# Seven waits of a two-block transformer kernel set in another order

## The reference, cut to what matters

```python
def rmsnorm(x, g):
    y = xf * lax.rsqrt(jnp.mean(xf * xf, axis=-1, keepdims=True) + EPS)
    return (y * g)
def swiglu(u, w_gate_up, w_down):            # F = 2816, four times in all
    gate, up = jnp.split(u @ w_gate_up, 2, axis=-1)
    return (jax.nn.silu(gate) * up) @ w_down
# block 1
h = x + 0.5 * swiglu(rmsnorm(x), ...)                       # ffn0
h = h + merged(rmsnorm(h)) @ w_mix_out                      # mix
h = h + memory_cross_attention(rmsnorm(h), rmsnorm(mem))    # xq, xo
h = h + 0.5 * swiglu(rmsnorm(h), ...)                       # ffn1
x = rmsnorm(h)
# block 2, layer 0: delta rule and memory attention, then FFN; layer 1: windowed attention
x = x + concat(gated_delta_rule(...), memory_attention(...)) @ w_out[0]   # qkv, gz, wo0
x = x + swiglu_2(rms_norm(x), ...)                          # ffn2
kv = rms_norm(x) @ w_kv ; shared_k = apply_partial_rope(k, cos, sin)
x = x + concat(sliding_window_attention(...), memory_attention(...)) @ w_out[1]   # q1, mq1, wo1
x = x + swiglu_2(rms_norm(x), ...)                          # ffn3
return rms_norm(x)
```

## Time and profile before

| | before |
|---|---|
| median of three runs | 1583.55 us (1582.07 to 1584.06) |
| profiled execution | 1582.77 us, span 1580.9 us |
| PE busy | 1538.4 us, 97% of the span |
| POOL busy | 1179.8 us, 75% |
| ACT busy | 836.7 us, 53% |
| DVE busy | 585.6 us, 37% |
| mean granted PE clock | 0.993 |
| DMA | 259.77 MB, mean 164 GB/s |

### The profile page before, as it was taken

The page is one execution under the profiler, slowest core; times in us unless marked ns, Lnnn a source line. Parts: engine busy times, 40 slices in busy tenths (PEclk is TensorE's granted clock), DMA queues, the critical chain, the costliest instruction groups (busy, mean ns, idle before and its releaser), DMA issues.

```text
span 1580.9 us, 21595 instructions
## 1 busy us (share of the span) xinstructions
PE 1538.4 (97%) x8592; PEld 1333.2 (84%) x8592; DVE 585.6 (37%) x992; ACT 836.7 (53%) x1310; POOL 1179.8 (75%) x508
## 2 busy tenths in 40 slices
PE   9999999999999999999999999999999998999997
PEld 7888789999888889878888888987888787778886
DVE  3111019356885612331231686452115246311101
ACT  6444464375666445365454685445444375554443
POOL 8889688888667889388878876627887872288893
PEclk9999999999999999999999999999999999999999
DMA  7555555565645555265555543015555451255551
GB/s 266 188 181 201 163 193 182 184 202 188 199 134 184 171 177 189 85 212 186 182 194 193 183 154 116 2 62 177 186 183 200 150 174 54 86 181 187 185 198 43
DMA packets 71859, 259.77 MB, mean 164 GB/s; under 512 B 7984, under 2 KB 8784, under 8 KB 71504
## 3 DMA queue, kind: packets, MB, share of 16 engines
q1 hardware_dynamic: 69408, 250.44, 47.8%
q10 hardware_dynamic: 2352, 7.96, 1.4%
HBM read 257.29 MB, written 1.08 MB: 163 GB/s over the span
## 4 chain that ended last, share of the span: by engine, by line
PE 84%; DVE 6%; POOL 5%; ACT 4%; issue 1%; POOLq 0%; ACTq 0%; DVEq 0%
PE bank L551 14%; PE bank L553 14%; PE bank L552 14%; PE bank L521 5%; PE bank L523 5%; PE bank L522 5%; POOL w_lo L436 5%; PE bank L581 4%; PE bank L583 4%; PE bank L582 4%; PE bank L694 1%; ACT w_hi L1323 1%; PE bank L1073 1%; PE bank L1094 1%; PE bank L1241 1%
## 5 line engine op out<-in xcount | busy, mean ns | idle before, releaser
L436 POOL TENSOR_TENSOR w_lo<-raw,w_hi 128x1024 fp32r<-128x1024 f32 x469 | 1132.8, 2443 | 345.2 <-ACT w_hi L1323 345.0
L1323 ACT ACTIVATE w_hi<-raw 128x1024 fp32r<-128x1024 f32 x474 | 486.8, 1057 | 379.1 <-PE bank L553 182.4
L551 PE MATMUL bank<-w_hi,u_hi 128*128 128x512 f32 x880 | 349.6, 397 | 7.8 <-POOL w_lo L436 7.8
L553 PE MATMUL bank<-w_hi,u_lo 128*128 128x512 f32 x880 | 343.9, 391 | 0.0
L552 PE MATMUL bank<-w_lo,u_hi 128*128 128x512 f32 x880 | 343.5, 390 | 0.0
L551 PEld LDWEIGHTS bank<-w_hi,u_hi 128*128 128x128 f32 x880 | 165.6, 188 | 43.7 <-POOL w_lo L436 9.4
L521 PE MATMUL bank<-u_hi,w_hi 128*128 128x256 f32 x688 | 197.8, 287 | 1.7 <-DVE ones_at L2366 1.7
L553 PEld LDWEIGHTS bank<-w_hi,u_lo 128*128 128x128 f32 x880 | 165.6, 188 | 35.4
L523 PE MATMUL bank<-u_hi,w_lo 128*128 128x256 f32 x688 | 195.4, 284 | 0.0
L522 PE MATMUL bank<-u_lo,w_hi 128*128 128x256 f32 x688 | 195.3, 284 | 0.0
L552 PEld LDWEIGHTS bank<-w_lo,u_hi 128*128 128x128 f32 x880 | 165.8, 188 | 32.7
(11 more groups left out here) (418 smaller groups left out, 2096.1 us busy)
## 6 DMA issues: line engine op xcount, KB each, us to landing
raw<-in_w SPq DMA_DIRECT2D x474, 512.0 KB, 4.4
bc<-acs_scratch ACTq DMA_DIRECT2D x8, 512.0 KB, 5.8
mem_t<-in_mem ACTq DMA_DIRECT2D x2, 1024.0 KB, 6.2
out<-out_t SPq DMA_DIRECT2D x4, 256.0 KB, 2.8
xf<-in_x ACTq DMA_DIRECT2D x1, 512.0 KB, 8.2
xf<-in_x SPq DMA_DIRECT2D x1, 512.0 KB, 8.8
lvl<-in_lvl ACTq DMA_DIRECT2D x1, 448.0 KB, 5.4
band<-in_band ACTq DMA_DIRECT2D x1, 256.0 KB, 5.4
```

Source lines behind the costliest of these rows:

```text
L436: nc.gpsimd.tensor_tensor(w_lo[:, q % RAW, :], raw[:, q % RAW, :], w_hi[:, q % HI, :].bitcast(F32), ALU.subtract).then_inc(split_done, 1)
L551: mm(b[:], hi[:, kt, a], w_hi[:, q % HI:q % HI + 2, c], start=kt == 0, stop=False)
L553: m = mm(b[:], lo[:, kt, a], w_hi[:, q % HI:q % HI + 2, c], start=False, stop=kt == KT - 1)
L1323: fn(w_hi[:, q % HI, :], raw[:, q % RAW, :], ACT.Copy).then_inc(hi_made, 1)
```

## The change

Seven edits, all in the order of waits and instructions; no operation is added or dropped except for one wait that becomes several.

1. `acc_stage`: PE waits for the low part of each held-back piece just ahead of its first use.
2. ffn2's end, ACT: the last `hid_hi` comes ahead of the sines, and five more weight high parts (`after(P0["ffn2_down"] + 4)`) too. DVE: the zeroing of kz and vz comes after the last `hid_lo`.
3. `qkv`: the wait for `picks` comes after the third row tile.
4. `half_tiles`: the second token half goes through k-tiles 0, 1, 2, 3, 6, 7, 4, 5.
5. `hi_part` gets `fed_to`: the weight high parts that were made after the eight high parts of u are made after the fourth. So for ffn1, ffn2 and ffn3; for mix one more of them comes even before the first.
6. Second attention, ACT: `normalise(i - 1)` comes ahead of head i's exponential.
7. Second attention, DVE: `rope(3)` comes ahead of `row_max(8)`.

```diff
@@ acc_stage @@
-                pe.wait_ge(split_done, P0[name] + n)
                 ready(n - 1)
                 for d in range(2):
                     for q in range(n - tail, n):
+                        if d == 0:
+                            pe.wait_ge(split_done, P0[name] + q + 1)
                         m = part(q, 0, d)
@@ PE, delta rule @@
-            pe.wait_ge(W["picks"], 2)
             for j in range(9):
                 row_stage("qkv", u_hi, u_lo, sub=(j, 1))
+                if j == 2:
+                    pe.wait_ge(W["picks"], 2)
...
-                    first, last = kt == (6 if s else 0), kt == (5 if s else 7)
+                    first, last = kt == 0, kt == (5 if s else 7)
...
-            half_tiles(1, (6, 7, 0, 1, 2, 3, 4, 5))
+            half_tiles(1, (0, 1, 2, 3, 6, 7, 4, 5))
@@ ACT @@
-            def hi_part(name, s, gain, dst=u_hi, turn=None):
+            def hi_part(name, s, gain, dst=u_hi, turn=None, fed_to=None):
+
                 for kt in range(KT):
+                    if kt == 4 and fed_to:
+                        after(fed_to)
...
                 after(d - 1)
+                if f == 2:
+                    hid_hi(f, 10)
                 if before_down:
                     before_down()
-                hid_hi(f, 10)
+                if f != 2:
+                    hid_hi(f, 10)
...
-            after(P0["gate_a"] - 5)
-            hi_part("mix", 0, "mix_norm")
-            after(P0["gate_a"] - 3)
+            after(P0["gate_a"] - 4)
+            hi_part("mix", 0, "mix_norm", fed_to=P0["gate_a"] - 3)
...
-            hi_part("ffn1", 0, "ffn2_norm")
-            after(P0["xo"] + 5)
+            hi_part("ffn1", 0, "ffn2_norm", fed_to=P0["xo"] + 5)
...
             def sines():
+                after(P0["ffn2_down"] + 4)
...
             for i in range(16):
+                if i:
+                    normalise(i - 1)
                 act.wait_ge(W["at_max"], h2 + i + 1)
...
-                if i:
-                    normalise(i - 1)
@@ DVE @@
-                dve.wait_ge(piece_done, P0["ffn2_down"] + 16)
-                for t in (kz, vz):
-                    v.memset(t[:], 0.0).then_inc(W["zeroed"], 1)
             ffn(2, beside_zeros)
+            dve.wait_ge(piece_done, P0["ffn2_down"] + 16)
+            for t in (kz, vz):
+                v.memset(t[:], 0.0).then_inc(W["zeroed"], 1)
...
+                if i == 6:
+                    rope(3)
                 if i + 2 < 16:
                     row_max(i + 2)
-                if i in (2, 6):
-                    rope(2 if i == 2 else 3)
+                if i == 2:
+                    rope(2)
```

More of the change, by code:

```diff
@@ L1801, in _ @@
             square("ffn2", 0)
-            hi_part("ffn2", 0, "ln_ffn_a")
-            after(P0["wo0"] + 5)
+            hi_part("ffn2", 0, "ln_ffn_a", fed_to=P0["wo0"] + 5)
             def ffn2_early():
@@ L1870, in _ @@
             square("ffn3", 0)
-            hi_part("ffn3", 0, "ln_ffn_b")
-            after(P0["wo1"] + 5)
+            hi_part("ffn3", 0, "ln_ffn_b", fed_to=P0["wo1"] + 5)
             def ffn3_early():
```

## The result

| | after |
|---|---|
| median of four runs | 1556.82 us (1555.94 to 1559.13) |
| kernel before, beside it | 1583.80 us median of four |
| ratio after to before | 0.9839 (95% interval 0.9826 to 0.9852) |
| profiled execution | 1559.13 us, span 1557.3 us, mean clock 0.997 |

Faster by 25.5 us by the ratio (23 to 28); forecast were 1561.0 us and 1556 to 1570.

What follows compares the result with a forecast made beforehand. TensorE (PE) was taken as the bound, busy 97% of the span, leaving only its waits and clock to win. Terms summed to 23.1 us, less 0.6 given back: 1583.55 - 22.5 = 1561.0 us, range 1556 to 1570.

Steps and rivals of the forecast that it cites:

- tails, first and third FFN: Ends of the first and third FFN's down projections: piecewise waits remove two PE waits of 0.94 us, 1.9 us.
- ffn2's end: End of ffn2's down projection: with the sines later, PE's 3.31 us wait goes entirely, plus 1.7 us of clock.
- picks: First qkv row tile: PE's 1.74 us wait on DVE's ones_at goes, plus 1.7 us of clock, 3.4 us.
- wo0's order: Delta rule's output: high part released two tiles earlier, 1.36 us off PE's 1.92 us wait, plus 1.7 us of clock.
- ffn1 to ffn3: Starts of the three FFNs: low part 1.0 us earlier, PE back 0.9 us earlier each, 2.7 us; bounds 0 and 3.1.
- mix: Start of mix: earlier weight high parts shorten the first gap, but later adds delay PE; net loss 0.65 us.
- attention: Second attention: normalising and rotation moved earlier leave 3.1 of 9.0 us idle, 5.9 us won, plus 1.7 us of clock.
- clock steps: Four PE stretches at the lower clock, 1.7 us each, vanish with the gaps ahead of them.
- Rival (c): Everything goes as walked and mix's gaps shrink too: 1557.6 us, chance 0.10.
- A gap that goes takes its clock loss along: PE's clock: assumed that removing an idle gap also removes the lower-clock stretch behind it, 1.7 us each.
- Rival (a): Waits go but clock steps stay, meeting remaining gaps elsewhere: 16.3 us won, 1567.2 us; chance 0.27 shared with another rival.
- the 0.6 that I gave back: Whole kernel: 0.6 us taken off the summed gain for a clock step one of the remaining gaps may find.

Runs made afterwards that it cites:

- x_tails: Changed kernel with PE again waiting once, for the last low part, ahead of a down projection's held-back pieces: 1561.28 us, ratio to before 0.9869.
- x_picks: Changed kernel with the wait for the one-hot columns (picks) again ahead of the first qkv row tile: 1560.35 us, ratio to before 0.9863.
- y_norms: Changed kernel with weight high parts again behind all eight high parts of u in ffn1, ffn2 and ffn3, mix left changed: 1560.07 us, ratio 0.9868.
- the second measurement: Changed kernel run again unaltered, beside the kernel before: medians 1557.50 and 1581.18 us, ratio 0.9851.
- x_ffn2end: Changed kernel with ACT's sines and DVE's zeroing at ffn2's end in their old places, piecewise waits kept: 1558.50 us, ratio to before 0.9849.
- y_att: Changed kernel with the second attention's old order on both ACT (normalising) and DVE (rotation): 1566.42 us, ratio to before 0.9909.
- z_before: The kernel before the change, run once more unaltered: 1581.51 us, ratio to before 0.9997.
- z_order: Changed kernel with wo0's second token half again in k-tile order 6, 7, 0, 1, 2, 3, 4, 5: 1558.58 us, ratio to before 0.9850.

## Why the prediction was right, step by step

| term | predicted, us | measured, us | from |
|---|---|---|---|
| tails, first and third FFN | 1.9 | 2.5 | 1.25 each, x_tails |
| ffn2's end | 3.3 | 3.5 | PE's starts, before and after |
| picks | 1.7 | 1.9 | gap 1.74 and the start behind it, x_picks |
| wo0's order | 1.4 | 1.3 | 1.92 to 0.60 |
| ffn1 to ffn3 | 2.7 | 2.9 | y_norms |
| mix | -0.65 | -0.2 | PE's starts, before and after |
| attention | 5.9 | 7.4 | 9.1 over the stage, less 1.7 for its step |
| clock steps | 6.8, less 0.6 | 5.3 | 1.5, 1.6, 1.7 and 1.7, less 1.2 at kv |
| last turn at the higher clock | 0 | 0.6 | PE's starts, before and after |
| sum | 22.5 | 25.2 | last matmul: 25.2 |

The last turn has no term in the prediction. The step at the rotation is put at its full 1.7 us; if it cost less, the attention's gaps are worth as much more. The execution gives 23.6, for the slower write at its end. By the runs' medians it is 27.0, by the ratio 25.5, in the second measurement 23.7: two executions compared part by part don't say which of these is the change's.

**The gaps** went where the walk had them, by the instruction it named; that each term came back alone when its part was undone shows it. ffn2's end is the closest walk. DVE, ACT and POOL there, after:

```profile
1210.55 2.37 DVE L2610 TENSOR_SCALAR ang<-ang 128x256 f32<-128x256 f32 x1
1212.96 2.37 DVE L2611 TENSOR_SCALAR ang<-ang 128x256 f32<-128x256 f32 x1
1215.37 0.29 DVE L2612 TENSOR_SCALAR ang<-ang 128x256 f32<-128x256 f32 x1
...
1232.79 0.68 DVE L1939 TENSOR_TENSOR h_lo<-bank,h_hi 128x512 fp32r<-128x512 f32 x1
...
1216.48 0.42 ACT L1825 ACTIVATE cs<-ang 128x256 f32<-128x256 f32 x1 [3.11 <-DVE ang L2614]
...
1217.93 28.99 POOL L436 TENSOR_TENSOR w_lo<-raw,w_hi 128x1024 fp32r<-128x1024 f32 x12 [2.75 <-ACT w_hi L1325]
```

Shifted by the 9.4 us won up to there, the walk said ACT back at 1216.6, POOL at 1217.7, the last hidden low part at 1233.6; the rows have 1216.48, 1217.93 and 1232.79. Seven of DVE's ten last angle steps took 2.4 to 2.5 us, the two-source ones too (three in 7.58 us at 1202.94), and the three behind POOL's pause 0.29 to 0.43. That agrees with the rule of the Trainium skill (SBUF — State Buffer, Who interferes with whom) for both kinds of step, the single-source ones and those with two SBUF inputs.

What was wrong there is the booking, which changed the total by 0.2 us only: the sum gave the sines edit 3.31 us and a step, and the piecewise waits nothing at this place, though it used them itself to cover a last low part 1 us late (1.55 by the row: 11 low parts from 1217.93 end at 1244.5, the tail starts at 1242.97). x_ffn2end shows what that hid: with the waits in, the edit is worth 0.95 us, a third of it the zeroing's move on DVE.

**Sizes off.** ffn1 to ffn3: each turn of x was to be 0.3 us late for DVE's later add. In ffn3 the add ran from 1360.90 to 1361.58 and the turn began at 1361.64, with no bracket, but 0.41 us after the start of the matmul ahead of it; in the kernel before it was 0.24. In all 0.2 us are lost there, near the 0.3. The 2.9 us lie within the bounds of 0 to 3.1. Attention: 3.1 us were to remain (0.1, 0.8, 0.6, 1.1, 0.5), and 2.4 do (0, 0.87, 0.18, 0.81, 0.49). y_att's own waits there are 8.9 us, so 6.6 of its 7.4 are waits; the last 0.8 are stalls too small for a row, which I hadn't walked. Mix: the edit against itself costs 0.2 and not 0.65. The first gap came out as walked (1.56, predicted 1.6), but the turn lost 0.35 us (no bracket) instead of 0.5 and the product behind it 0.5 (bracket 0.41) instead of 0.7. The tails were put at their brackets, 0.94 us, and are worth 1.25 each. Rival (c)'s gain isn't there either, though its 1557.6 is the number nearest to the median.

**The clock** is the step that was right for a reason that doesn't hold as stated. "A gap that goes takes its clock loss along" is true of the two traces compared, but z_before, x_picks and z_order show that a gap of 1.7 to 2.2 us carries a step in some executions only, and kv shows that two gaps of about 1 us can carry one. Rival (a), the steps stay, is out: four and five in the traces of before against one in each of the changed kernel's, the stretch at the end of the span left out. But what a removed gap of this length brings is its length and a share of a step's 1.2 to 1.7 us, and the 0.6 that I gave back was too small for the two traced executions (1.2 each) and about right for a mean (5/13 of 1.2 is 0.5). That the forecast's total is near is in part luck: before's trace had four steps and after's one, where other executions of before have, by their spans, two to five, and the gaps were worth more than booked (attention, tails).

## What to carry to other kernels

When two edits act on one wait, walk each without the other: here the piecewise waits alone were worth 2.5 of 3.5 us, and the edit that looked like the main one added 0.95. A wait for several producers ahead of work that uses them one by one is worth splitting before any producer is made faster. Count a gap by its length, and what the clock loses behind it as a chance read from several executions, not from one trace.

## What the runs showed that I had not expected

- A step of the clock to 1.2 GHz lasts 3.41 us in every trace, wherever it falls, except the one at the end of the span. 1.7 us of full speed are lost in it, and PE comes out 1.2 to 1.7 us late. Whether one follows a given gap changed between executions of the same program (the 2.2 us at mix: none at 1580.9 us of span, one at 1582.0). Most of the spread of the kernel before, 1577.0 to 1582.1 us of span, is this, if the groups are read rightly.
- The gaps at these edits repeat to 0.03 us between executions. They, and not medians with 2 us of interval, resolve an edit of 0.5 us. Not all of the program repeats so: a wait near 11 us, on DVE's low parts of u, is 0.45 to 1.56 us in nine traces and under 0.4 in five, and PE's starts behind it lie up to 0.4 us apart from one trace to another. So the shifts given here are taken over a stretch and not from the start of the span.
- The output's last write varies by itself: the span ends 5.1 to 5.4 us behind the last matmul in twelve traces, 6.7 to 7.0 in two, in which the third output transfer's issue comes some 2 us later.
